# Half of the output projection moved into the second mixer's loop, with the residual added by Pool

## What is computed

```
o_gla = (rmsnorm(o, gla_norm_w) * jax.nn.silu(g)...).reshape(bsz, seq_len, GLA_VW)      # 512 features
y = rmsnorm(y.reshape(bsz, seq_len, SSD_INNER) * jax.nn.silu(z), ssd_norm_w)            # 512 features
mix = jnp.concatenate([o_gla, y], axis=-1).astype(dtype)
out = mix @ w_out                                                                       # 1024 x 1024
...
h = h + m                                                                               # m is out
h = h + peer(rmsnorm(h, norm2_w[l]), peer_wq[l], peer_k1[l], peer_k2[l], peer_u[l], peer_v[l])
```

## Time and profile before

| | |
|---|---|
| median of 3 runs | 2124.3 us (2109.77 to 2129.03) |
| time of the profiled execution | 2123.39 us |
| its span, first to last instruction | 2121.2 us |
| PE busy | 2028.3 us (96%) |
| DVE / Pool / ACT busy | 1209.6 / 1132.3 / 623.0 us |
| mean granted TensorE clock | 0.974 |

### The profile page before, as it was taken

One profiled execution on the slowest core, in us unless ns is written; L12 is line 12 of the kernel. 1 busy time (PEld: TensorE's weight loads), 2 busy tenths in 40 slices (PEclk: granted clock), 3 DMA queues, 4 the chain that ended last, 5 costly groups with the idle time before them and its releaser, 6 DMA issues. The chain is left out here.

```text
span 2121.2 us, 31685 instructions
## 1 busy us (share of the span) xinstructions
PE 2028.3 (96%) x12559; PEld 1848.1 (87%) x12559; DVE 1209.6 (57%) x2223; ACT 623.0 (29%) x971; POOL 1132.3 (53%) x697
## 2 busy tenths in 40 slices
PE   5999998699899999999999999998999999999996
PEld 3578777577799999999999999997999999999995
DVE  2325364733699787778433332113577777777773
ACT  2224112310242323232323333223333333333331
POOL 0023220200447788888888888884566666666200
PEclk8999998879999999999999999999999999999998
DMA  3097102011235565556555555777999999999961
GB/s 145 2 341 263 40 31 85 1 66 62 94 103 125 124 125 124 125 124 132 127 130 125 124 117 125 157 181 239 325 317 322 320 319 320 321 318 318 328 199 46
DMA packets 231787, 365.34 MB, mean 172 GB/s; under 512 B 92129, under 2 KB 157170, under 8 KB 231026
## 3 DMA queue, kind: packets, MB, share of 16 engines
q1 hardware_dynamic: 153330, 294.43, 42.2%
q0 software_dynamic: 78336, 69.25, 16.6%
HBM read 290.21 MB, written 73.38 MB: 171 GB/s over the span
## 5 line engine op out<-in xcount | busy, mean ns | idle before, releaser
L801 PE MATMUL bank<-xh,usp 128*128 128x288 f32 x4320 | 754.4, 296 | 1.4 <-DVE xl L1429 1.4
L1659 POOL DMA_INDIRECT gates_scratch<-gate_val,gate_at x384 | 667.4, 1738 | 133.8 <-issue 115.8
L896 PE MATMUL bank<-W,vsp 128*128 128x448 f32 x3072 | 636.6, 369 | 9.2 <-DVE W L1558 9.2
L801 PEld LDWEIGHTS bank<-xh,usp 128*128 128x128 f32 x4320 | 636.7, 189 | 3.2 <-DVE xl L1429 1.9
L896 PEld LDWEIGHTS bank<-W,vsp 128*128 128x128 f32 x3072 | 577.8, 188 | 67.8 <-issue 9.4
L801 PE MATMUL bank<-xl,usp 128*128 128x288 f32 x2160 | 462.5, 296 | 0.0
L801 PEld LDWEIGHTS bank<-xl,usp 128*128 128x128 f32 x2160 | 348.0, 189 | 0.0
L1441 DVE TENSOR_TENSOR usp<-ring,usp 128x1024 fp32r<-128x1024 f32 x120 | 146.6, 1222 | 335.0 <-ACT usp L1052 334.7
L1553 DVE TENSOR_TENSOR vsp<-ring,vsp 128x1024 fp32r<-128x1024 f32 x128 | 156.8, 1226 | 177.1 <-ACT vsp L1137 176.7
L1681 POOL DMA_INDIRECT picked<-in_v,row_index x128 | 150.1, 1173 | 193.5 <-DVE acc L1572 167.8
L1078 ACT ACTIVATE gl<-bank 128x288 f32<-128x288 f32 x256 | 91.3, 409 | 522.0 <-PE bank L801 521.7
(11 more groups left out here) (245 smaller groups left out, 1590.0 us busy)
## 6 DMA issues: line engine op xcount, KB each, us to landing
ring<-in_u SPq DMA_DIRECT2D x128, 512.0 KB, 3.7
ring<-in_v SPq DMA_DIRECT2D x128, 512.0 KB, 5.4
hidden_scratch<-gl SPq DMA_DIRECT2D x128, 288.0 KB, 2.2
xn<-hidden_scratch SPq DMA_DIRECT2D x128, 224.0 KB, 5.7
G<-gates_scratch SPq DMA_DIRECT2D x120, 224.0 KB, 4.7
gates_scratch<-zero SPq DMA_DIRECT2D x32, 768.0 KB, 8.9
ring<-in_wproj SPq DMA_DIRECT2D x36, 512.0 KB, 3.8
gates_scratch<-gate_val,gate_at POOLq DMA_INDIRECT x384
```

The lines of the kernel that those rows point to most:

```text
L801: mm = pe.matmul(bank[b + y][:, 0:PHALF], w, src[:, k, y * PHALF:(y + 1) * PHALF], start=(k == 0 and w is hi and src is xh), stop=(k == KT ...
L896: mm = pe.matmul(bank[(k + 4) % 8][:, 0:TA], w, W[:, n % 4, z, :], start=(n == 0 and w is hi and z == 0), stop=(n == NE - 1 and w is lo))
L1659: pool.indirect_dma_start(gates_flat, bass.IndirectOffsetOnAxis(ap=gate_at[0:r, i, x:x + 1], axis=0), gate_val[0:r, i, hh, x - hh * TOPK:x ...
```

## The change

`project_out` is split. `project_gla(k)` makes GLA's half of output tile `k` into banks 6 and 7 and runs inside the SSD loop, once in each of the five token tiles, between `pre(i + 1)` and `y(i)`. The other three run after the loop: one before the sums of the normalisation, two behind them. ACT copies each half out of PSUM into SBUF (`gla_out`, memory that the GLA mixer no longer uses), at the end of its work for a token tile. Pool adds it to `h` when the input is loaded again (`x_added`). `project_ssd(k)` then makes only SSD's half, and DVE adds that to `h` as before.

Banks 6 and 7 are taken for this, so `ssd_banks` of odd tiles becomes (0, 1, 3) in place of (3, 6, 7): banks 0 and 1 now serve every tile, and `pre(i)` waits for `ecb_ready >= i` and `z_ready >= i` (ACT and DVE have read them for tile i - 1). The weights are loaded as halves: a slot holds GLA's 512 rows for two output tiles, and later SSD's 512 rows for two. Four loads come ahead of the loop and four behind the reloads of the input. PE waits for all eight copies (`half_copied`) before the first `project_ssd`, because `to_state(4, c)` uses banks 6 and 7. Four semaphores of GLA's normalisation become one, `gvar_step`, with the same order.

```diff
-        ssd_banks, CUM_AT = [(0, 1, 2), (3, 6, 7)], SG * P
+        ssd_banks, CUM_AT = [(0, 1, 2), (0, 1, 3)], SG * P
...
+            for j in range(4):
+                sp.wait_ge(proj_done, N_FEAT - 3 + j)
+                load_out(j, 0)
...
+            for j in range(4):
+                sp.wait_ge(half_done, 2 * j + 2)
+                load_out(j, 1)
...
+                if i >= 1:
+                    pe.wait_ge(ecb_ready, i)
+                    pe.wait_ge(z_ready, i)
...
+            def project_gla(k):
+
+                pe.wait_ge(ring_loaded[k // 2], 16 * (N_FEAT // 4 + 1))
+                if k >= 1:
+                    pe.wait_ge(half_copied, k)
+                for x in range(2):
+                    for c in range(GH):
+                        a = k % 2 * (D // 2) + c * P
+                        mm = pe.matmul(bank[6 + x][:, 0:HALF], ring[:, k // 2, a:a + P], mix[:, c, x * HALF:(x + 1) * HALF],
+                                       start=(c == 0), stop=(c == GH - 1))
+                mm.then_inc(half_done, 1)
+
+            pe.wait_ge(g_mixed, GH)
             pre(0)
             for i in range(TILES):
                 r = rows(i)
                 if i < 4:
                     pre(i + 1)
+                project_gla(i)
...
+            project_gla(TILES)
             pe.wait_ge(y_copied, TILES)
             for k in range(4):
                 norm_sum(1, k)
-            project_out(N_FEAT + 1, 0)
+            project_gla(TILES + 1)
+            project_gla(TILES + 2)
+            pe.wait_ge(half_copied, KT)
             pe.wait_ge(normed, norm_base[1] + 4)
             for k in range(KT):
                 if k >= 2:
                     norm_sum(2, k - 2)
-                if k >= 2:
-                    project_out(N_FEAT + k, 0)
-                project_out(N_FEAT + k, 1)
+                project_ssd(k)
...
+            def copy_gla_out(k):
+                act.wait_ge(half_done, k + 1)
+                for x in range(2):
+                    ins = act.activation(gla_out[k][:, x * HALF:(x + 1) * HALF], bank[6 + x][:, 0:HALF], ACT.Copy)
+                ins.then_inc(half_copied, 1)
...
+                if i >= 1:
+                    copy_gla_out(i - 1)
+            copy_gla_out(TILES - 1)
+            copy_gla_out(TILES)
             norm(1, lambda k: act.wait_ge(yz_ready, k + 1))
+            copy_gla_out(TILES + 1)
+            copy_gla_out(TILES + 2)
             norm(2, lambda k: act.wait_ge(proj_dve, k + 1))
...
-            dve.wait_ge(x_reloaded, 16 * KT)
             for k in range(KT):
                 n = N_FEAT + k
+                dve.wait_ge(x_added, k + 1)
                 dve.wait_ge(proj_done, n + 1)
...
+            pool.wait_ge(x_reloaded, 16 * KT)
+            for k in range(KT):
+                pool.wait_ge(half_copied, k + 1)
+                pool.tensor_tensor(h[:, k, :], h[:, k, :], gla_out[k], ALU.add).then_inc(x_added, 1)
```

More of the change, by code:

```diff
@@ L225, in build @@
         Ef = E[:, :, :].rearrange("p a b -> p (a b)")
+        gla_out = [Ef[:, k * T:(k + 1) * T] if k < 6 else sg[:, k - 6, :] for k in range(KT)]
         wv_sb = Ef[:, 0:KT * GH * DV].rearrange("p (k n) -> p k n", k=KT)
@@ L308, in build @@
         proj_done, proj_act, proj_dve = map(sem, ["proj_done", "proj_act", "proj_dve"])
+        half_done, half_copied, x_added = map(sem, ["half_done", "half_copied", "x_added"])
         sq_ready, sq_used, root_ready, normed = map(sem, ["sq_ready", "sq_used", "root_ready", "normed"])
@@ L321, in build @@
             sem, ["s_zero", "local_done", "s_updated", "inter_done", "o_copied"])
-        gsq_ready, gsum_done, gvar_ready, groot_ready, grstd_ready, gbc_done, g_normed, g_mixed = map(
-            sem, ["gsq_ready", "gsum_done", "gvar_ready", "groot_ready", "grstd_ready", "gbc_done", "g_normed", "g_mixed"])
+        gsq_ready, gsum_done, gvar_step, g_normed, g_mixed = map(
+            sem, ["gsq_ready", "gsum_done", "gvar_step", "g_normed", "g_mixed"])
         x_reloaded, conv_link, conv_done, xc_ready, tr_done, tr_copied = map(
@@ L430, in _, with load_out @@
             sp.dma_start(Ssm[:, :, :, :], d["s_gla"]).then_inc(sgla_loaded, 16)
-            for n in range(12, N_FEAT + 4):
+            for n in range(12, N_FEAT):
                 load_w(n)
+            def load_out(j, ssd_part):
+                n = N_FEAT + 2 * j
+                sp.dma_start(ring[:, j, :].rearrange("p (a c) -> p a c", a=2),
+                             d["wproj"][n:n + 2, :, ssd_part * (D // 2):(ssd_part + 1) * (D // 2)].rearrange("a p c -> p a c")
+                             ).then_inc(ring_loaded[j], 16)
+            for j in range(4):
+                sp.wait_ge(proj_done, N_FEAT - 3 + j)
+                load_out(j, 0)
             sp.wait_ge(s_updated, PROMPT_CHUNKS)
@@ L444, in _ @@
                 sp.dma_start(h[:, k, :], d["xT"][:, k, :]).then_inc(x_reloaded, 16)
-            for n in range(N_FEAT + 4, N_FEAT + KT + 4):
-                load_w(n)
+            for j in range(4):
+                sp.wait_ge(half_done, 2 * j + 2)
+                load_out(j, 1)
+            for n in range(N_FEAT + KT, N_FEAT + KT + 4):
+                sp.wait_ge(proj_done, N_FEAT + 2 * (n % 4) + 2)
+                sp.dma_start(ring[:, n % 4, :], d["wproj"][n]).then_inc(ring_loaded[n % 4], 16)
             sp.wait_ge(h_updated, TILES)
@@ L675, in _ @@
             mm.then_inc(gsum_done, 1)
-            pe.wait_ge(grstd_ready, 1)
+            pe.wait_ge(gvar_step, 3)
             pe.wait_ge(proj_act, N_FEAT)
@@ L682, in _ @@
                                    ident[0:rows(i), 0:rows(i)], start=True, stop=True)
-            mm.then_inc(gbc_done, 1)
+            mm.then_inc(gvar_step, 1)
             pe.wait_ge(o_copied, TILES)
@@ L704, in pre @@
                 b = ssd_banks[i % 2]
+                if i >= 1:
+                    pe.wait_ge(ecb_ready, i)
+                    pe.wait_ge(z_ready, i)
                 if i >= 2:
-                    pe.wait_ge(ecb_ready, i - 1)
                     pe.wait_ge(wx_ready, i - 1)
@@ L762, in _, with project_ssd @@
                     to_state(i, 0)
[L764 to L768, removed]
-                for x in range(2):
[L770 to L778, removed]
+            def project_ssd(k):
+                n = N_FEAT + k
+                if k % 2 == 0:
+                    pe.wait_ge(ring_loaded[k // 2], 16 * (N_FEAT // 4 + 2))
+                wait_proj_evacuated(pe, n)
+                for x in range(2):
+                    for c in range(4):
+                        a = k % 2 * (D // 2) + c * P
+                        mm = pe.matmul(bank[2 * (n % 2) + x][:, 0:HALF], ring[:, k // 2, a:a + P],
+                                       mix[:, 4 + c, x * HALF:(x + 1) * HALF], start=(c == 0), stop=(c == 3))
+                mm.then_inc(proj_done, 1)
+            project_gla(TILES)
             pe.wait_ge(y_copied, TILES)
@@ L1015, in _ @@
             act.activation(gsq, mix[:, 0:GH, :], ACT.Square).then_inc(gsq_ready, 1)
-            act.wait_ge(gvar_ready, 1)
-            act.activation(gstat[:, 0, :], gstat[:, 0, :], ACT.Sqrt).then_inc(groot_ready, 1)
+            act.wait_ge(gvar_step, 1)
+            act.activation(gstat[:, 0, :], gstat[:, 0, :], ACT.Sqrt).then_inc(gvar_step, 1)
             conv_out(7)
@@ L1318, in _ @@
             dve.tensor_scalar(gstat[0:rows(4), 0, 4 * GH:], bank[4][0:rows(4), 4 * GH:5 * GH], 1.0 / DV, EPS, ALU.mult,
[L1319 to L1322, removed]
+                              ALU.add).then_inc(gvar_step, 1)
+            dve.wait_ge(gvar_step, 2)
+            dve.reciprocal(gstat[:, 1, :], gstat[:, 0, :]).then_inc(gvar_step, 1)
+            dve.wait_ge(gvar_step, 4)
             for hh in range(GH):
```

## The result

The changed kernel takes 2098.11 us in the median of four runs (2087.74 to 2103.1), the kernel before 2119.58 us in its four (2109.77 to 2129.03). The ratio is 0.9894, 95% interval 0.9854 to 0.9935: the medians are 21.5 us apart, where 2099 us was forecast. Twelve later runs of the changed kernel beside seventeen of the kernel before have medians of 2098.08 and 2114.53 us, 16.4 us apart (0.9926, 0.9900 to 0.9951). The profiled execution has a span of 2101.1 us against 2121.2, 20.1 us less. The profile shows where they come from, stage by stage.

What follows compares the result with a forecast made beforehand. The prediction took PE's row of matmuls and Pool's scatter, both starting from the mixers, as the bound. +1.4 - 3 + 3.4 - 26.9 = -25.1 us from 2123.4 gave 2098.3, with the median 0.9 higher 2099 us; range 2087 to 2112.

Steps and rivals of the forecast that it cites:

- The gain arrives whole: From the mixers to the kernel's end: a microsecond won before about 530 us should reach the end whole.
- The rival in which it gets lost at the scatter: At the `v` stage: PE comes early and waits for Pool's last scatter; half lost gives 2111 us; chance 0.06.
- Part 1, the loop: SSD loop: halves fill PE's waits for DVE, clock stays 1.00, cycles of 9.65 us; `y(4)` starts 1.4 us later.
- Part 2, `y(4)`: `y` of tile 4: starts at clock 1.00 behind a half; -3 us, the middle between -6 and 0.
- Part 3, to the first SSD half: From the end of `y(4)` to the first SSD half: copies delay it to 21.1 us against 17.7, +3.4 us.
- Part 4, the rounds: Projection rounds: six lose eight matmuls each, 5.85 us instead of 9.84, and the first half gains 3.0; -26.9 us.
- The number: Whole kernel: terms sum to -25.1 us from 2123.4, giving a median of 2099 us, 1.2% faster.
- The slower rival: SSD loop: clock 0.50 from tile 0 to 4 makes the kernel 8 to 17 us slower, 2132 to 2141; chance 0.04.
- the rival in which the clock still drops in the loop: SSD loop: one tile at clock 0.50 gives 2108 us, two tiles 2115; chance 0.2.

Runs made afterwards that it cites:

- Halves ahead of `pre`: Changed kernel with each of the first four GLA halves placed ahead of `pre` instead of behind it (also written halves_ahead_of_pre); span 2108.9 us.
- All three together: own_banks plus half 5 spread through `y(4)`, half 0 ahead of `pre(1)`, half 6 ahead of the sums (also all_repairs); median 2102.6 us, 0.9933.
- Half 5 as one block: own_banks with half 5 as one block in the middle of `y(4)`, behind its fourth head; median 2093.76 us, 0.9891 of the kernel before.
- Pool waits: Changed kernel with Pool's eight adds started only after DVE's four scalings (also pool_hold); median 2090.09 us, 0.9893 of the kernel before.
- squares_first: Changed kernel with ACT making the normalisation's squares and root before copying half 5; median of ten runs 2089.68 us, 0.9891 of the kernel before.
- own_banks: Changed kernel with own banks for halves 6 and 7, squares and root before half 5's copy, Pool's adds after the scaling; median 2088.1 us, 0.9868.
- changed_again: The changed kernel as it is, profiled and timed again beside other kernels on one chip; median 2098.08 us, 0.9926 of the kernel before.
- spread half: Changed kernel with half 5 spread through `y(4)`, one matmul behind each of eight heads, instead of behind it (also interleave); span 2108.7 us.

## Why the prediction was right

**The gain arrives whole.** Right: -20.1 us at the first query, -20.1 at Pool's first scatter, -20.3 at the start of the `v` stage, -20.1 in the span. The rival in which it gets lost at the scatter is out.

**Part 1, the loop.** The mechanism was right: no wait, clock 1.00, starts 9.68 us apart where 9.65 was worked out. The size was +2.9 us instead of +1.4 (counted from `pre(0)`), and all of the difference lies ahead of `y(0)`, which came 2.9 us later than in the kernel before; from `y(0)` to `y(4)` it is 35.7 us in both. What I missed is that the new wait of `pre(1)` for ACT, which I had priced by its own length, drops the clock of the `pre` behind it: 3.27 us for a first line that takes 2.02. "Halves ahead of `pre`" and "All three together" put half 0 in that wait, and there the first line of `pre(1)` takes 1.95 us. In the other tiles the sum held waiting and clock together, as a cycle worked out at 1.00; "Halves ahead of `pre`" shows what they are worth there, 4.2 us a tile, 2.6 of waiting and 1.6 of clock.

**Part 2, `y(4)`.** -3.1 us, for the -3 that was a middle between two ends. The start at clock 1.00 was right, and so was the price of the full clock (8.5 us forecast for the whole, 8.6 by the heads of "Half 5 as one block"). That the clock would be lost again after 4 us was not worked out; the -3 was a choice, and that it fits is luck. The drop came 4 to 6 us into this `y(4)` in the runs that leave it whole, with 10.0 to 11.5 us for the whole. What I wouldn't have guessed is that wide matmuls in it don't keep the clock either.

**Part 3, to the first SSD half.** The step that failed in size: +3.4 forecast, +6.3 measured. The sums came at 7.2 us, half 6 at 11.4, the end of the last copy at 21.5: that path was right to 0.5 us. But the scaling ended at 23.8 and not at 19.2 to 22.1. I had allowed for at most two of Pool's adds beside it. The input landed later than forecast, so the adds began at 10.4 us and not at 9, and four of the eight were left when the scaling began. And the two queues stretch each other: the adds end at 453.4, 455.3 and 457.2 us, and the scalings some 0.6 us behind each of them, which reads as each operation waiting for the other engine's running one. Both proceed at 1.9 us an operation instead of 0.75 and 1.43, and all four scalings met an add. Three doses fit: no add beside the scaling 3.07 us ("Pool waits"), two at its start 4.50 ("Halves ahead of `pre`"), four 7.54. With Pool held the path was the one I had named, ACT's last copy, at 21.5.

The Trainium skill ("SBUF — State Buffer", section "Who interferes with whom") calls the shared pair of ports an exclusive lock under which the later one fully blocks. The 7.54 against 3.07 us with nothing changed but Pool's timing agrees.

I had weighed this rule at 1.0 us at most; it cost 2.4 us, and another 1.5 by the clock, since PE's wait before the first SSD half was 3.24 us and not the forecast 1.

**Part 4, the rounds.** 5.85 us as forecast; the whole was -25.3 instead of -26.9, because the first half ran at the low clock (5.70 instead of 4.15 us) behind the 3.24 us wait.

**The number.** Three parts fell short, by 1.5, 2.9 and 1.6 us; against them stand 0.1 us of part 2 and the 0.9 us before `pre(0)`, which are scatter. The sum, -25.1, was 5 to 6 us too good. That the forecast median was met within 1 us is luck: it was counted from 2124.3 us, a median of three runs that lay high. The fourth run brought it to 2119.58, and three later sets of thirteen to seventeen runs have medians of 2114.5 to 2115.5.

**The slower rival** needed the clock at 0.50 all through the loop. It was at 1.00 from 387 to 424 us. So the rival in which the clock still drops in the loop didn't come either. What it warned of acted beside the loop: at `pre(1)` and at the first SSD half, each behind a wait that the change made, and in `y(4)`, where PE never stood still.

## What to carry to other kernels

Independent work pays where an engine waits, and it can pay twice on PE, since behind a wait of 2.6 us the matmuls were 1.6 us slower here in most tiles, though not in all; so count the waits that the move creates (shared banks, handshakes, a port) at that same double price. Before giving elementwise work to Pool because it is idle, look at which DVE operations with two SBUF inputs run beside it, and start Pool behind them if they are on the path. A win inside a stage is worth only what the next wait leaves of it: twice here an earlier end uncovered a wait of about the same length.

## What was not expected of the hardware

**The `v` stage has two lengths.** Its 3072 records on PE take 624.3 to 625.5 us in five profiled executions (pool_hold, squares_first, own_banks twice, changed_again) and 636.5 to 637.7 in the other eight. The changed kernel shows both, 637.60 and 625.28. In neither does PE wait, and the granted clock is 1.00 in both; the same stretch in the changed kernel, and then in pool_hold:

```profile
1600.00:1750.00 150.00, 150.00 (x727) 136.26 (x726) 110.08 (x127) 50.23 (x61) 96.18 (x72) 1.00 0.93 321
```

```profile
1600.00:1750.00 150.00, 150.00 (x742) 139.00 (x741) 113.06 (x130) 50.44 (x62) 94.88 (x71) 1.00 0.95 327
```

742 records in the time of 727, and the two stretches of 150 us behind it have the same counts to within one. This is 12 us in whole times, more than any repair here, and it is why the experiments are judged by their stages. The transfers are close in both, 321 and 327 GB/s. What sets it stays open; no experiment was made on it.

**A busy PE can lose the clock.** In the spread half it dropped at 433 us with PE busy without a gap for 46 us, 0.99 to 1.00 until then. Which property of the work decides stays open: a closed block of eight wide matmuls got it back (in the middle of `y(4)`, and behind it in the kernels that have it there), eight spread ones did not keep it, and the time from the start of `y(4)` to the drop was about 4, 4, 6, 8 and 11 us (changed kernel, own_banks, halves_ahead_of_pre, interleave, all_repairs).
